# Eleven raw weight slots, ten rounded ones, and a longer lead of the first token tile

## The chip, the cores and the metric

The kernel runs on one core of a Trainium2 chip. The metric is the device time of one execution in microseconds (us), the median of several. The engines go by their names in the profile: PE (TensorE, matmuls; PEld its weight loads), DVE (VectorE), ACT (ScalarE), POOL (GpSimd) and SP (SyncE), whose queue issues the loads of the weights.

## What is computed

Two stacked models share one activation of 256 tokens by 1024 columns. The first has four layers, the second two:

```python
for i in range(DEPTH):                       # 4 layers
    q, k, v, ... = split_cols(x @ w_in[i], ...)          # 3144 or 2560 columns
    mix = attention(q, k, v)                 # selected keys, dilated, or causal blocks
    mo = memory_attention(qm, mk, mv)        # mk, mv = mem_n @ w_mem_kv[i]
    mixed = concatenate([mix, mo]) @ w_out[i]
    x = layer_norm(ALPHA * x + mixed, ...)
    x = layer_norm(ALPHA * x + swiglu(x, w_gate_up[i], w_down[i]), ...)
for l in range(DEPTH_2):                     # 2 layers
    u = rms_norm(x, norm_pre[l]) @ w_in_2[l]             # three attentions on parts of u
    y = gated sum of the three branches @ w_br_a, w_br_b, w_br_c
    x = x + rms_norm(y @ w_out_2[l], norm_post[l])
    x = x + sigmoid(x @ w_ple_gate[l]) * (p[l] @ w_ple_proj[l])
```

All inputs are float32. The result is the last `x`.

## The kernel before

Every product of activations with weights is made of **units**. A unit is up to two row tiles of 128 rows (`UK = 2`) of a column chunk of at most 512 columns. The kernel has 624 of them, numbered in program order. SP loads a unit into one of `RAW = 10` slots; ACT rounds it to float32r in one of `SPLIT = 8` slots (`w_hi`, line 1213); POOL subtracts the rounded from the raw values, in the raw slot itself (`w_lo`, line 1185). PE then makes three products of each row tile: high activations by high weights (L1419), high by low (L1420), low by high (L1426; L1422 where the tile was just turned). The 256 tokens are two tiles of 128, so each unit has two halves on PE, which this text calls the t0 half and the t1 half. A t0 half waits for `w_lo` of its unit; a t1 half comes later in PE's queue.

Slots come free by the t1 half alone: the load of unit n waits for the t1 half of unit n-10, and the rounding of unit n for that of n-8. Unit n's t0 half is planned behind the t1 half of unit n-5 (`LAG = 5`), so t0 runs five units ahead of t1 in the long stages. There are two exceptions. After a norm, the t0 halves of the first `SPLIT` units need no t1 half of the new activations, since the second tile is still being normed. And a chunk that is `closing` (the last one before a norm: the second 512 columns of `w_out`, `w_down`, `w_out_2` and `w_ple_gate_2`) lets the t0 halves of its last two units go one and two units further ahead, so that the first token tile's norm runs on DVE while PE still has t1 halves. After it PE turns the normed rows (L1366) and begins the next weights.

The order on every engine is made when the program is built. `plan()` writes tasks with costs, priorities and what they wait for, and `Plan.arrange()` places them one after the other by earliest begin. Each engine then executes its list in that order, waiting on semaphores. PE's four `acc` banks hold at most two chunks of each token tile, so after a norm at most eight t0 halves of four-unit chunks stand ahead of the first t1 half.

At the seam of `w_gate_up` and `w_down`, the last gate and up chunks have 256 columns (eight narrow units), and the norm's gain and bias are loaded by SP (L1136, L1140) just behind the first load of `w_down`.

Of the kernel before, what the change touches and what calls it, by code (L numbers as in the profile page):

```python
# [42 lines left out]

CHUNK = 512
UK = 2
RAW = 10
SPLIT = 8
LAG = 5
CROSS = 120
FIRST_CONSTANTS = 3  # L50
# [242 lines left out]
class Plan:  # L293
# [135 lines left out]
    def open_chunk(self, weight, k_tiles, acts, spec, fed=((), ()), clear=((), ()), banks=None, hold=((), ()),  # L429
# [8 lines left out]
        for k0 in range(0, k_tiles, UK):  # L438
            n = len(self.units)
            nk = min(UK, k_tiles - k0)  # L440
            u = Unit(n, k0, nk, rows[k0] if rows else k0, ch, weight)
            size = nk * width
            u.load = self.task("SP", "load", u, size * 512 / 300, None,
                               [self.units[n - RAW].mm[1]] if n >= RAW else [], prio=1 if n >= RAW else -3 if n == 0 else -1, lat=2000)
            u.split = self.task("ACT", "split", u, 195 + 0.835 * size, "hi_ready",
                                [u.load] + ([self.units[n - SPLIT].mm[1]] if n >= SPLIT else []),
                                prio=1 if n else -1)
            if n == 0:
                u.low = self.task("DVE", "low", u, 100 + 1.03 * size, "lo_ready_dve", [u.split], prio=-1)
            else:  # L450
                u.low = self.task("POOL", "low", u, 240 + 2.12 * size, "lo_ready", [u.split])
            for t in range(T):
                feed = [self.fed[name][r][base + k0 + i] for r in (range(T) if flip else (t,)) for i in range(nk)]
                u.fed[t] = [k for k in feed if k is not None]
                after = [u.low, *[k.it.hi if k.kind == "take" and not flip else k for k in u.fed[t]]]
                if n:
                    after.append(self.units[n - 1].mm[t])
                if t:
                    after.append(u.mm[0])
                else:  # L460
                    last = n - LAG
                    if n < self.normed + SPLIT:
                        last = min(last, self.normed - 1)
                    if closing and k0 >= k_tiles - 2 * UK:
                        last = len(self.units) - 1 - (k0 - (k_tiles - UK)) // UK - LAG - 2 + 1
                    after += [self.units[last].mm[1]] if last >= 0 else []
                room = None
                if k0 == 0:
                    room = ("acc", banks[t])
                    after += hold[t]  # L470
                u.mm[t] = self.task("PE", "products", (u, t), 3 * nk * pe_cost(width), "mm_done", after,
                                    prio=0.8 + 0.1 * t if closing else 1 + t, room=room)
            self.units.append(u)
            ch.units.append(u)
# [464 lines left out]
def build(nc, a, out):  # L939
# [5 lines left out]
    with ExitStack() as ctx:  # L945
# [8 lines left out]
        with landing:  # L954
            raw = landing.enter_context(nc.sbuf_tensor("raw", [P, RAW, UK, CHUNK], F32))
        rounded = ExitStack()
        with rounded:
            w_lo = rounded.enter_context(nc.sbuf_tensor("w_lo", [P, RAW, UK, CHUNK], F32R))
        ctx.enter_context(nc.sbuf_tensor("raw_or_lo", [P, RAW, UK, CHUNK], F32))
        w_hi = sb("w_hi", [P, SPLIT, UK, CHUNK], F32R)  # L960
        xT_hi = sb("xT_hi", [P, 8, N], F32R)
# [163 lines left out]
        def _(sp):  # L1125
# [16 lines left out]
            def load_unit(u):  # L1142
                if u.u >= RAW:

# [34 lines left out]
        def _(pool):  # L1179
            def low_part(u):  # L1180
                ch, slot, r = u.chunk, u.u % SPLIT, u.u % RAW

# [914 lines left out]
```

How the kernel before makes its waits and increments, by code:

```python
        @block.sync  # L1124
# [1 line left out]
            def load_gain(g):  # L1126
                slot = g.slot
                if g.last is not None:
                    for done in g.last.rest:
                        sp.wait_ge(S["stage"], done.n)
                for done in g.apart:
                    sp.wait_ge(S[done.sem], done.n)
                name, row = g.g
                src = a[name] if row is None else a[name][row]
                to = Y[:, 0, :] if slot else gain[:, 0, :]
                sp.dma_start(to, src.partition_broadcast(P)).then_inc(gain_landed[slot], 16)
                if g.b[0]:
                    name, row = g.b
                    src = a[name] if row is None else a[name][row]
                    sp.dma_start(gain[:, 1, :], src.partition_broadcast(P)).then_inc(gain_landed[slot], 16)
# [1 line left out]
            def load_unit(u):  # L1142
                if u.u >= RAW:
                    sp.wait_ge(S["mm_done"], p.units[u.u - RAW].mm[1].n)
                ch = u.chunk
                src = u.weight[u.row * P:(u.row + u.nk) * P, ch.col:ch.col + ch.width]
                sp.dma_start(raw[:, u.u % RAW, 0:u.nk, 0:ch.width],
                             src.rearrange("(k p) n -> p k n", p=P)).then_inc(unit_landed[u.u % RAW], 16)
# [15 lines left out]
                elif k.kind == "save_rel_rows":  # L1165
                    n = P // REL_PIECES
                    sp.wait_ge(S["rel_rows_made"], 1)
                    sp.dma_start(rel_rows[:, n * k.it:n * k.it + n, :], rel_made.unsqueeze(1)
```

## Time and profile before

| | |
|---|---|
| median of 3 executions | 1910.05 us |
| lowest and highest | 1909.97, 1911.69 us |
| span of the profiled execution | 1906.5 us |
| PE busy | 1865.8 us (98%) |
| POOL busy | 1516.2 us (80%) |
| ACT, DVE busy | 945.2 us (50%), 798.1 us (42%) |
| DMA | 330.54 MB, mean 173 GB/s |

The span runs from the first to the last instruction; the median is 3.5 us longer than it. A matmul's length in the profile reaches past the start of the next one, because matmuls are pipelined, so short waits of PE are partly hidden in its busy time. The number in square brackets at the end of a row of the timeline is the engine's idle time before it and what ended it.

### The profile page before, as it was taken

Reading aid. Unit: us, or ns where it says so; the run is one execution under the profiler, and the core shown is the slowest. Engines: PE = TensorE matmul, PEld = TensorE weight load, DVE = VectorE, ACT = ScalarE, POOL = GpSimd, SP = SyncE. Lnnn points to the kernel's source line nnn. Section 1 sums busy time; section 2 is a strip of 40 time slices with the busy share of each in tenths; the row PEclk is TensorE's granted clock in tenths of the full one; section 3 lists DMA queues with packets and bytes.
Section 4 is the critical chain, followed back from the end, with each engine's and each line's share of the span. In section 5 each row is a group of like instructions: output and inputs, shape, how many; then the busy total and the mean of one; then the engine's idle time right before and its main releaser. Section 6 shows DMA issues by size and latency. Waiting matters only on the chain.

```text
span 1906.5 us, 27403 instructions
## 1 busy us (share of the span) xinstructions
PE 1865.8 (98%) x9610; PEld 1529.7 (80%) x9610; DVE 798.1 (42%) x1933; ACT 945.2 (50%) x1501; POOL 1516.2 (80%) x1330
## 2 busy tenths in 40 slices
PE   8999999999999999999999999999999999999999
PEld 7878888877888887788887778887887887788877
DVE  6774110456111245411056641106857344455534
ACT  4564444454444445444435544434656654555743
POOL 7768979885897977797987779797686887777785
PEclk9999999999999999999999999999999999999999
DMA  8445656555666554465655456655564564556453
GB/s 292 137 146 178 187 164 223 179 176 145 184 193 214 188 172 149 144 188 164 223 150 157 152 166 187 208 169 174 178 182 122 161 209 152 162 170 178 130 173 111
DMA packets 184558, 330.54 MB, mean 173 GB/s; under 512 B 12221, under 2 KB 44521, under 8 KB 184425
## 3 DMA queue, kind: packets, MB, share of 16 engines
q1 hardware_dynamic: 176512, 323.21, 55.0%
q10 hardware_dynamic: 7912, 5.59, 1.0%
q8 instruction: 80, 1.31, 0.3%
q14 instruction: 54, 0.43, 0.1%
HBM read 325.35 MB, written 3.41 MB: 172 GB/s over the span
## 4 chain that ended last, share of the span: by engine, by line
PE 84%; POOL 6%; DVE 4%; DMA 3%; ACT 2%; issue 1%; SPq 0%; DVEq 0%; ACTq 0%
PE acc L1419 24%; PE acc L1420 23%; PE acc L1426 21%; POOL w_lo L1185 6%; PE tps L1366 4%; PE acc L1441 2%; PE acc L1422 2%; PE ops L1483 2%; PE tps L1459 2%; DMA raw<-in_w_down 1%; PE acc L1390 1%; PE acc L1392 1%; PE acc L1391 1%; DMA raw<-in_w_mem_kv 1%; PE ops L1378 1%
## 5 line engine op out<-in xcount | busy, mean ns | idle before, releaser
L1185 POOL TENSOR_TENSOR w_lo<-raw,w_hi 128x512 fp32r<-128x512 f32 (+2 forms) x1242 | 1475.3, 1225 | 349.9 <-ACT w_hi L1213 348.7
L1213 ACT CAST w_hi<-raw 128x1024 fp32r<-128x1024 f32 (+3 forms) x624 | 615.6, 991 | 745.3 <-PE acc L1426 567.2
L1419 PE MATMUL acc<-w_hi,xT_hi 128*128 128x512 f32 (+1 forms) x1808 | 687.1, 384 | 4.9 <-ACT U L1247 2.9
L1420 PE MATMUL acc<-w_lo,xT_hi 128*128 128x512 f32 (+1 forms) x1808 | 666.6, 372 | 0.0
L1426 PE MATMUL acc<-w_hi,xT_lo 128*128 128x512 f32 (+2 forms) x1744 | 505.2, 371 | 0.0
L1419 PEld LDWEIGHTS acc<-w_hi,xT_hi 128*128 128x128 f32 x1808 | 341.4, 189 | 74.6 <-issue 15.2
L1420 PEld LDWEIGHTS acc<-w_lo,xT_hi 128*128 128x128 f32 x1808 | 342.2, 189 | 52.4
L1426 PEld LDWEIGHTS acc<-w_hi,xT_lo 128*128 128x128 f32 x1744 | 317.8, 189 | 58.2 <-DVE xT_lo L1696 1.1
L1756 DVE TENSOR_TENSOR H<-G,acc 128x512 f32<-128x512 f32 (+1 forms) x48 | 30.9, 643 | 335.5 <-PE acc L1426 335.5
L1419 PE MATMUL acc<-w_hi,hT_hi 128*128 128x512 f32 x352 | 139.5, 396 | 3.6 <-POOL w_lo L1185 3.4
L1420 PE MATMUL acc<-w_lo,hT_hi 128*128 128x512 f32 x352 | 137.2, 390 | 0.0
L1426 PE MATMUL acc<-w_hi,hT_lo 128*128 128x512 f32 x352 | 108.5, 389 | 0.0
L1749 DVE SCALAR_TENSOR_TENSOR acc<-x_rows,acc 128x512 f32<-128x512 f32 x32 | 22.2, 694 | 201.5 <-PE acc L1426 175.9
L1267 ACT ACTIVATE L<-L,neg_max 128x128 f32<-128x128 f32 (+2 forms) x208 | 96.2, 464 | 11.2 <-DVE neg_max L1943 8.5
L1419 PEld LDWEIGHTS acc<-w_hi,hT_hi 128*128 128x128 f32 x352 | 66.1, 188 | 21.6 <-issue 8.9
L1419 PE MATMUL acc<-w_hi,sT_hi 128*128 128x512 f32 (+1 forms) x200 | 78.9, 395 | 2.1 <-DVE MKV L1746 1.1
L1426 PEld LDWEIGHTS acc<-w_hi,hT_lo 128*128 128x128 f32 x352 | 66.1, 188 | 14.1
L1420 PE MATMUL acc<-w_lo,sT_hi 128*128 128x512 f32 (+1 forms) x200 | 77.3, 387 | 0.0
L1420 PEld LDWEIGHTS acc<-w_lo,hT_hi 128*128 128x128 f32 x352 | 66.1, 188 | 12.7
L1985 DVE COPY PT<-tps 128x384 f32<-128x384 f32 (+1 forms) x96 | 53.3, 575 | 42.2 <-PE tps L1459 31.1
L1696 DVE TENSOR_TENSOR hT_lo<-tps,hT_hi 128x512 fp32r<-128x512 f32 (+1 forms) x48 | 31.1, 648 | 92.3 <-ACT hT_hi L1221 92.3
L1196 POOL TENSOR_TENSOR L<-L,recips 128x128 f32<-128x128 f32 (+1 forms) x84 | 42.5, 529 | 27.4 <-DVE recips L1973 27.3
(210 smaller groups left out, 1993.5 us busy)
## 6 DMA issues: line engine op xcount, KB each, us to landing
raw<-in_w_gate_up SPq DMA_DIRECT2D x160, 512.0 KB, 3.9
raw<-in_w_in SPq DMA_DIRECT2D x104, 512.0 KB, 3.8
raw<-in_w_down SPq DMA_DIRECT2D x88, 512.0 KB, 3.7
raw<-in_w_out SPq DMA_DIRECT2D x48, 512.0 KB, 3.6
raw<-in_w_in_a SPq DMA_DIRECT2D x32, 512.0 KB, 3.6
raw<-in_w_in_b SPq DMA_DIRECT2D x20, 512.0 KB, 3.7
raw<-in_w_mem_kv SPq DMA_DIRECT2D x16, 512.0 KB, 4.2
raw<-in_w_gate_up SPq DMA_DIRECT2D x32, 256.0 KB, 2.8
```

The lines of the kernel that those rows point to most:

```text
L1185: ins = nc.gpsimd.tensor_tensor(w_lo[:, r, i, 0:ch.width], raw[:, r, i, 0:ch.width], w_hi[:, slot, i, 0:ch.width].bitcast(F32), ALU.subtract)
L1196: ins = nc.gpsimd.tensor_tensor(part, part, by, ALU.mult)
L1213: nc.scalar.copy(w_hi[:, u.u % SPLIT, 0:u.nk, 0:u.chunk.width], raw[:, u.u % RAW, 0:u.nk, 0:u.chunk.width]).then_inc(S["hi_ready"], 1)
L1267: ins = nc.scalar.activation(part, part, ACT.Exp, bias=neg_max[:, slot, c:c + 1], accum_out=sums[:, slot, c:c + 1])
L1366: ins = nc.tensor.transpose(tps[0:width, k.slot[0], P * i:P * i + P], rows(src)[:, t, col:col + width], ident[:])
L1419: nc.tensor.matmul(o, hi[:, tok], wh, start=first_k, stop=False)
L1420: ins = nc.tensor.matmul(o, hi[:, tok], wl, start=False, stop=False)
L1422: ins = nc.tensor.matmul(o, lo[:, tok], wh, start=False, stop=last_k)
L1426: ins = nc.tensor.matmul(acc[:, bank, 0:ch.width], act_tile(ch.acts, u.k0 + i)[1][:, P * t:P * t + P], w_hi[:, u.u % SPLIT, i, 0:ch.width] ...
L1441: ins = nc.tensor.matmul(acc[:, k.slot[m], c], QT[base:base + n, qt, P * t:P * t + P], KT[kbase:kbase + n, kt, 0:c.stop - c.start], start= ...
L1459: ins = nc.tensor.transpose(tps[:, k.slot[0], P * i:P * i + P], lg[:, j, P * i:P * i + P], ident[:])
L1985: v.tensor_copy(PT[:, j, 0:blocks * P], tps[:, s.turn[j].slot[0], 0:blocks * P]).then_inc(S["t_taken"], 1)
```

## The change

Three numbers change: 11 raw slots instead of 10, 10 rounded slots instead of 8, and 1 KB per partition of SBUF set aside for DMA descriptors instead of the default 16 KB, which makes room for them (4 KB of each partition for a slot of either kind). The rule for closing chunks is rewritten: it now holds for all units of such a chunk, and the last one's t0 half is planned behind the t1 half of unit n-9, the one before it behind n-8, then n-7, n-6 and n-5.

```diff
-RAW = 10
-SPLIT = 8
+RAW = 11
+SPLIT = 10
+DMA_SCRATCH = 1024
...
-                    if closing and k0 >= k_tiles - 2 * UK:
-                        last = len(self.units) - 1 - (k0 - (k_tiles - UK)) // UK - LAG - 2 + 1
+                    if closing:
+                        last = min(last, n - max(LAG, SPLIT - 1 - (k_tiles - UK - k0) // UK))
...
-    nc = bacc.Bacc("TRN2", target_bir_lowering=False, num_devices=1)
+    nc = bacc.Bacc("TRN2", target_bir_lowering=False, num_devices=1, dynamic_dma_scratch_size=DMA_SCRATCH)
```

No instruction is added or taken away; the lists of all engines are ordered anew. Lines are numbered one higher in the new kernel. Three places show it.

**SP, the start of the program.** `raw` is a unit's slot, `in_w_mem_kv` the weights of the memory keys and values, `masks` to `sinks` constants. Before:

```order
10 L1148 DMA raw<-in_w_in_a 128x2x512 x2
11 L1148 DMA raw<-in_w_mem_kv 128x2x512 x2
12 L1164 DMA masks<-in_c_masks 128x1536
13 L1164 DMA knorm<-in_idx_kn_g 128x2x64
...
19 L1164 DMA sinks<-in_sw_sinks 128x16
20 L1148 DMA raw<-in_w_mem_kv 128x2x512 x2
```

Now:

```order
10 L1149 DMA raw<-in_w_in_a 128x2x512
11 L1149 DMA raw<-in_w_mem_kv 128x2x512 x3
12 L1165 DMA masks<-in_c_masks 128x1536
13 L1165 DMA knorm<-in_idx_kn_g 128x2x64
...
19 L1165 DMA sinks<-in_sw_sinks 128x16
20 L1149 DMA raw<-in_w_mem_kv 128x2x512
```

The third unit of `w_mem_kv` is now issued ahead of the eight constants; the fourth stays behind them. One more unit of `w_in_a` also stands ahead of the load of `mem`.

**PE, the end of `w_down` in layer 0.** `x_rows` are the first token tile's normed rows being turned, `hT` the activations of `w_down`, `MKV` the memory keys of the next layer. Before:

```order
1273 L1366 MATMUL tps<-ident,x_rows 128x128 x8
1274 L1419 MATMUL acc<-w_hi,hT_hi 128x512
...
1283 L1426 MATMUL acc<-w_hi,hT_lo 128x512 x2
1284 L1366 MATMUL tps<-ident,MKV 128x128 x4
```

Now:

```order
1259 L1367 MATMUL tps<-ident,x_rows 128x128 x8
1260 L1420 MATMUL acc<-w_hi,hT_hi 128x512
...
1279 L1427 MATMUL acc<-w_hi,hT_lo 128x512 x2
1280 L1367 MATMUL tps<-ident,MKV 128x128 x4
```

A half is five rows. Two t1 halves stood between the turned rows and the end of the stage, and now four do. Five stand between the last t0 half and the turned rows both times: seven t1 halves in all before, nine now. The same holds for the other three `w_down` and the two `w_out_2`; `w_out` of layer 0 has eight instead of seven, and `w_out` of layers 1 to 3 keep six, five and five.

**DVE, the end of `w_ple_gate_2` in the first of the two layers.** L1860 to L1863 add a chunk of one token tile into its bank, L1610 begins the first tile's norm, L1849 writes its normed rows. Before:

```order
1296 L1860 TENSOR_TENSOR acc<-acc,U 128x512
1297 L1862 TENSOR_TENSOR acc<-acc,x_rows 128x512
...
1302 L1860 TENSOR_TENSOR acc<-acc,U 128x512
1303 L1862 TENSOR_TENSOR acc<-acc,x_rows 128x512
1304 L1863 BN_STATS stats<-acc 128x6
1305 L1610 BN_AGGR small<-stats 128x2
...
1316 L1849 SCALAR_TENSOR_TENSOR tmp<-acc,small,gain 128x512 x2
1317 L1860 TENSOR_TENSOR acc<-acc,U 128x512
```

Now:

```order
1291 L1861 TENSOR_TENSOR acc<-acc,U 128x512
...
1294 L1861 TENSOR_TENSOR acc<-acc,U 128x512
1295 L1863 TENSOR_TENSOR acc<-acc,x_rows 128x512
1296 L1864 BN_STATS stats<-acc 128x6
1297 L1611 BN_AGGR small<-stats 128x2
...
1308 L1850 SCALAR_TENSOR_TENSOR tmp<-acc,small,gain 128x512 x2
1309 L1697 TENSOR_TENSOR xT_lo<-tps,xT_hi 128x4x128 x2
1310 L1861 TENSOR_TENSOR acc<-acc,U 128x512
```

Of the second token tile, one chunk's addition stood ahead of the first tile's norm, and now none does. On PE, the t0 halves of `w_ple_proj_2` and of all of `w_ple_gate_2` (ten units, 520 to 529) now stand ahead of the t1 half of unit 520; before, five t1 halves stood ahead of unit 528 and one more ahead of 529, so that four were left behind the last t0 half, where ten are now. The turned rows stand behind the fifth of the ten.

## Rows read from the trace of the kernel before

**Rows 1.** The page, 1: busy time of each engine.
```profile
PE 1865.8 (98%) x9610; PEld 1529.7 (80%) x9610; DVE 798.1 (42%) x1933; ACT 945.2 (50%) x1501; POOL 1516.2 (80%) x1330
```

**Rows 2.** The waits of PE, whole span: total us, times, longest.
```profile
PE tps L1366 <- DVE tmp L1849: 5.2, 2, 2.6
PE acc L1419 <- POOL w_lo L1185: 4.9, 15, 1.6
...
PE tps L1459 <- DVE L L2012: 4.2, 3, 1.7
```

**Rows 3.** Timeline of PE, end of w_down, layer 0: start, length, line.
```profile
343.13 0.61 PE L1426 MATMUL acc<-w_hi,hT_lo 128*128 128x512 f32 x2
...
344.49 0.61 PE L1426 MATMUL acc<-w_hi,hT_lo 128*128 128x512 f32 x2
...
349.03 1.05 PE L1366 MATMUL tps<-ident,x_rows 128*128 128x128 f32 x8
```

**Rows 4.** Timeline of PE, end of w_gate_up, layer 0: two neighbouring t1 halves.
```profile
277.67 0.62 PE L1426 MATMUL acc<-w_hi,xT_lo 128*128 128x512 f32 x2
...
279.77 0.62 PE L1426 MATMUL acc<-w_hi,xT_lo 128*128 128x512 f32 x2
```

**Rows 5.** The chain, 280 to 360 us: start, length, what.
```profile
280.42 6.54 DMA raw<-in_w_down
288.11 22.55 POOL w_lo L1185 x18
...
340.97 0.25 PE acc L1419
```

**Rows 6.** POOL by line, 288.2 to 343.1 us; PE's waits, 280 to 345 us.
```profile
L1185 POOL TENSOR_TENSOR w_lo<-raw,w_hi 128x512 fp32r<-128x512 f32 x44 | 55.0, 1294 | 2.2 <-ACT w_hi L1213 2.2
...
PE acc L1419 <- POOL w_lo L1185: 1.0, 4, 0.4
```

**Rows 7.** Timeline of DVE and PE, end of layer 3.
```profile
1284.97 0.70 DVE L1749 SCALAR_TENSOR_TENSOR acc<-x_rows,acc 128x512 f32<-128x512 f32 x1 [13.58 <-PE acc L1426]
...
1309.56 1.41 DVE L1849 SCALAR_TENSOR_TENSOR tmp<-acc,small,Y 128x512 f32<-128x512 f32 x2
...
1297.01 1.93 PE L1366 MATMUL tps<-ident,tmp 128*128 128x128 f32 x8 [2.56 <-DVE tmp L1849]
...
1310.56 1.18 PE L1366 MATMUL tps<-ident,tmp 128*128 128x128 f32 x8
```

**Rows 8.** PE by windows of 8 us: busy (count), granted clock, DMA.
```profile
1294.00:1302.00 8.00, 5.44 (x22) 0.79 0.57 208
1596.00:1604.00 8.00, 5.29 (x19) 0.80 0.55 194
```

**Rows 9.** Timeline of DVE and PE, end of the first w_ple_gate_2.
```profile
1591.46 0.70 DVE L1860 TENSOR_TENSOR acc<-acc,U 128x512 f32<-128x512 f32 x1 [10.94 <-ACT acc L1247]
...
1598.47 1.41 DVE L1849 SCALAR_TENSOR_TENSOR tmp<-acc,small,gain 128x512 f32<-128x512 f32 x2
...
1590.69 0.62 PE L1426 MATMUL acc<-w_hi,xT_lo 128*128 128x512 f32 x2
...
1599.37 1.29 PE L1366 MATMUL tps<-ident,tmp 128*128 128x128 f32 x8 [2.62 <-DVE tmp L1849]
...
1609.38 1.04 PE L1366 MATMUL tps<-ident,tmp 128*128 128x128 f32 x8
```

**Rows 10.** Timeline of PE, the start: the fourth of its products.
```profile
45.57 0.47 PE L1419 MATMUL acc<-w_hi,mT_hi 128*128 128x512 f32 x1 [1.57 <-POOL w_lo L1185]
```

**Rows 11.** Timeline of DVE and POOL in the differential attentions.
```profile
1342.26 0.75 DVE L2012 SCALAR_TENSOR_TENSOR L<-L,recips 128x128 f32<-128x128 f32 x2
...
1652.59 2.86 DVE L2012 SCALAR_TENSOR_TENSOR L<-L,recips 128x128 f32<-128x128 f32 x2
...
1652.61 5.22 POOL L1185 TENSOR_TENSOR w_lo<-raw,w_hi 128x512 fp32r<-128x512 f32 x4 [2.17 <-ACT w_hi L1213]
```

**Rows 12.** The page, 3: the queue of the weights; packets, MB, share of time.
```profile
q1 hardware_dynamic: 176512, 323.21, 55.0%
```

## The prediction

> **What bounds the kernel now.** I read the page first: PE is busy for 1865.8 of 1906.5 us [rows 1], so only its waits and its clock can be won. Then the waits of PE over the whole span, grouped by what ended them [rows 2]: DVE's `tmp` 5.2 us in two waits, POOL's `w_lo` 4.9 us in 15, the attention's `L` 4.2 us in three. Then the timeline around the seams that the change reorders, and the granted clock there. Since the next matmul starts before the shown end of the one ahead, a shown wait is some 0.16 us longer in truth (0.39 us shown against starts 0.23 us apart, in the timeline around the row of [rows 10]).
>
> The unit of account is a half of a 512-wide unit on PE: 344.49 - 343.13 = 1.36 us [rows 3], so 2.72 us a unit, while POOL makes its `w_lo` in 55.0 / 44 x 2 = 2.50 us [rows 6]. POOL gains only 0.22 us a unit on PE. That small margin is what decides the sum: where the new order wants `w_lo` earlier than before, POOL must have started earlier by as much.
>
> **The start, -0.9 us.** PE waits 1.57 us for POOL before the third unit of `w_mem_kv` [rows 10], 1.8 us in truth, and its load stands behind eight constants. It now stands ahead of them; the fourth stays behind. The fourth is wanted about one t0 half of this narrow product, 0.9 us, later than the third was, so I take 1.8 - 0.9 = 0.9 us as still waited for. Bounds: 0 if the constants only push the wait to the fourth unit whole, -1.8 if it goes. The extra load of `w_in_a` ahead of `mem` is covered, since DVE takes up `mem` late.
>
> **End of `w_down` in layers 0 to 2, +0.6 us each.** What starts POOL: the load of the second `w_down` unit was issued at 280.42, right behind the t1 half of the unit ten before it, took 6.54 us, and after ACT's rounding POOL works from 288.11 on [rows 5] without a pause worth the name: 2.2 us idle in the 55 [rows 6]. With an eleventh slot the load waits for the t1 half one unit earlier. Neighbouring t1 halves start 2.10 us apart here (279.77 - 277.67 [rows 4]; the units are narrow), so the whole row of POOL comes 2.1 us earlier. The four waits of PE at the head of `w_down` (1.0 us shown, 1.6 in truth [rows 6]) then go. At the tail, the last unit's t0 half starts at 341.03 now (the chain has PE at it from 340.97 [rows 5]), 0.4 us after its `w_lo`, so just in time. The new order has two more t1 halves behind it: wanted at 341.0 - 1.6 - 2 x 1.36 = 336.7, while POOL can give it at 341.0 - 2.1 = 338.9. So a wait of 2.2 us appears there. The turned rows then end at 338.9 + 1.36 + 9 x 1.36 + 0.9 = 353.4, if all nine t1 halves (five and four) stand behind the last t0 half as the order has it. The same sum for now is 341.0 + 1.36 + 7 x 1.36 + 0.9 = 352.8: +0.6 us, three times, +1.8 in all. The norm of the first tile ends well ahead in both. Bounds: -1.6 each if POOL keeps up (the head's waits go, no tail wait), +2.7 each if POOL doesn't start earlier at all (rival B).
>
> **End of layer 3, -2.1 us.** Here the norm is longer than the t1 halves behind it. PE waits 2.56 us for `tmp`, and again it turns rows at 1310.56 just when DVE has the second tile's `tmp` of 1309.56; DVE began the first tile at 1284.97 [rows 7] and works on without a pause. The window 1294 to 1302 has a granted clock of 0.79 [rows 8], that is, some 3.4 us of it at the lower level of 1.2 GHz and 1.7 us lost. Wait and clock cost 2.56 + 0.16 + 1.7 = 4.4 us, but DVE's row of work ends them both, and all that moves it is the end of the t0 halves, which comes earlier by POOL's 2.1 us. So -2.1 us; the two further t1 halves behind the last t0 half (2 x 1.36 = 2.7 us) fill the gap and more. Bounds: 0 (POOL doesn't start earlier) and -2.7.
>
> **First `w_ple_gate_2`, -3.0 us.** The gap is 2.62 us in front of the turned rows at 1599.37 [rows 9], and the clock of 1596 to 1604 is 0.80 [rows 8]: 2.62 + 0.16 + 1.6 = 4.4 us lost. From DVE's first addition at 1591.46, right behind the last t0 half, to PE's turning it is 8 us, of which four t1 halves (5.4 us) cover the most. Now ten t1 halves stand behind the last t0 half, five of them ahead of the turned rows: 6.8 us of cover. The gap shrinks to 8.1 - 6.8 = 1.3 us, too short to lower the clock if it goes as with the waits of 1.7 us (no window shows a drop there). 4.4 - 1.4 = 3.0 us won. The second turning at 1609.38 hangs on the last t1 half; it is wanted some five t0 halves after the first new one (6.9 us) and is ready 7 to 8 us after the last t1 half, so it takes back at most 1 us. Bounds: -4.4 (gap closes, as DVE no longer serves another chunk first) and -1.5 (POOL gives the last two units late: it has ten `w_lo` to make with PE using t0 halves alone, at 1.36 us each against its 2.50).
>
> **Other seams, 0.** `w_out` in layers 1 to 3 keeps its order, and the second `w_ple_gate_2` and the two `w_out_2` have no such gap today. New banks or reads cost nothing.
>
> **The scratch of 1 KB, 0.** It is a reservation. All 323 MB of weights go by a queue of the kind hardware_dynamic [rows 12], and GpSimd issues no load. If it did slow the loads, each `w_down` load would land later than 6.54 us after its issue, and the forecast would become rival B. Nothing in it can gain.
>
> **Attentions, 0, between -4 and +4.** PE's list is the same in layers 1 and 2; in the differential attention the scores start a little earlier and fewer t1 halves cover what follows. POOL, two units ahead, meets DVE at other moments. That matters: a pair of L2012 takes 0.75 us at 1342.26, but 2.86 us at 1652.59, when POOL has a row of `w_lo` from 1652.61 on [rows 11]. Each pair costs 2.1 us more when it collides; 3 of 8 do so by the timeline (a fourth in part), and PE's 4.2 us for `L` [rows 2] hang on them. The Trainium skill ("SBUF — State Buffer", "Who interferes with whom") says that the shared port pair of DVE and GpSimd is an exclusive lock; by that rule a DVE operation with two SBUF inputs is held up whole while a GpSimd instruction holds the lock, and the trace agrees (2.86 against 0.75 us). That makes rival C.
>
> **Sum.** -0.9 + 1.8 - 2.1 - 3.0 = -4.2 us against the span of 1906.5, so 1902.3. The median is 3.5 us above the span; 1905.8 is the predicted time. About 0.2% (3.8 us) is what a measurement of this kernel can tell from no change, so that the bound of faster lies at 1906.2, hardly above it.
>
> **The rivals.**
>
> A, POOL keeps up at the ends of `w_down`. For it: it has 80% of the span as busy time, and two more rounded slots let it take in whatever idle time it has earlier in `w_gate_up`. Against it: raw slots, not rounded ones, set when `w_down` lands [rows 5]. -1.6 x 3, -0.9 to -1.8, -2.1, -4.4: -12 to -13, and the middle between this and the forecast is 1901; the full case 1897.5.
>
> B, the slower one: POOL gets no head start in `w_down`. The transfer of 6.54 us [rows 5] lies beside other loads and is issued one slot sooner only to queue; if it lands at 287 as before, the tail's last `w_lo` comes at 340.6 as before, and behind its t0 half there are now nine halves instead of seven: +2.7 us in each of three layers, +8.1. The end of layer 3 gives 0, the gate -2, the start -0.9: 1910.05 + 5.2 = 1915.3. It decides against me from the point where POOL's start moves by less than 1.5 us (the forecast's three ends then cost over 3.6 us together). Against it: the load is issued at once when its slot comes free, today.
>
> C, collisions in the attentions. Two more pairs of L2012 that meet POOL's row, on the path, are +4.2 us and eat the gain: 1909 to 1911. For it: which ones meet depends on a microsecond, and the margins of PE's turning behind them are small. Against: it can as well go the other way.
>
> D, hardly an effect: the change doesn't do at the gate what its order says, because there, as in layer 3 [rows 7], DVE's row of both norms sets when PE goes on: the second turning at 1609.38 [rows 9] stays, and the cover of ten halves is filled for nothing. Then -0.9 + 1.8 - 2.1 = -1.2 us, 1908.9, or up to 1911 if layer 3 stays too.
>
> **How the numbers follow.** Forecast 0.40 (1903 to 1908.5, 60% of it below 1906.2), A 0.20 (1897 to 1903), C 0.18, D 0.08, B 0.14 (1914 to 1917). Faster: 0.24 + 0.20 = 0.44, and 0.01 for C going the other way, 0.45. Slower 0.14, same the remaining 0.41. The range of 1898.0 to 1912.0 leaves out B and the low end of A, nearly 2 in 10.
>
> **What would show it.** In the new trace the load of the second `w_down` unit lands about 2.1 us earlier against the t1 halves of `w_gate_up`, PE's four waits at the head of `w_down` are gone, and two or so of 1 us or more stand ahead of the last two t0 halves of it. The gap of 2.56 us in layer 3 is under 1 us, that of 2.62 us about 1.3, and the granted clock is 1.00 in both places. The wait in the start is 1 us or less. The prediction is wrong in its main step if POOL's start in `w_down` moves by less than 1.5 us, or if no wait appears at its tail; it is wrong in size if the differential attentions' waits for `L` move by over 2 us.

## The result, and the profile after

The changed kernel takes 1915.43 us (median of 18 executions, 1909.5 to 1918.5) and the kernel before 1909.28 us (18 executions, 1907.1 to 1912.0): 1.0027 of the time before, with a 95% interval of 1.0021 to 1.0034. It is slower by some 5 to 6 us, beyond the 0.2% that the prediction set as its bound. The profiled execution has a span of 1914.9 us, 8.4 us above the 1906.5 us of before. It took 1916.74 us, 1.3 us more than the median. A time is here 1.8 us above the span of the same execution, so the one of before took some 1908.3 us, 1.0 us less than its median. That is why the spans differ by 8.4 us and the medians by 6.1. The size of each seam below holds for the profiled execution only.

The page of the kernel after, busy time, which answers to [rows 1]:

```profile
PE 1869.1 (98%) x9610; PEld 1531.1 (80%) x9610; DVE 804.1 (42%) x1933; ACT 943.5 (49%) x1501; POOL 1514.3 (79%) x1330
```

And its waits of PE over the whole span (total us, times, longest), which answer to [rows 2]:

```profile
PE acc L1420 <- POOL w_lo L1186: 7.9, 16, 1.7
...
PE acc L1420 <- DVE MKV L1747: 2.5, 3, 1.7
...
PE tps L1460 <- DVE L L2013: 2.3, 2, 1.3
PE acc L1427 <- DVE xT_lo L1697: 2.0, 1, 2.0
PE acc L1420 <- ACT xT_hi L1222: 1.7, 3, 0.7
...
PE tps L1367 <- DVE sT_lo L1697: 1.5, 2, 0.8
```

The wait for `tmp` (5.2 us before) has shrunk to 0.3 us as intended, but the wait for POOL's `w_lo` has grown from 4.9 to 7.9 us, and others have come or grown: `xT_lo` and `sT_lo` were not in the list of before, and `xT_hi` had 0.2 us. PE does the same work; what the change bought at two places it gave back at others.

To see where, I compared the two traces at the end of the t1 half of the same unit, stage by stage. A t1 half's end is in PE's timeline as the last row of L1427 (L1426 before) of that unit. Each number is how much that end has moved (us, + is later) against the same end in the kernel before, over the stage alone. The last four columns are experiments told below. The borders are units behind which the order of halves is the same in all columns. The columns come from one execution each: against the medians of their kernels, the profiled one of the slots alone is 2.3 us long, that of the gate alone 1.3 us short, that of the late gains 1.2 and of both 2.8 us short.

| stage | after | slots alone | gate alone | late gains | gate and late gains |
|---|---|---|---|---|---|
| start to end of `w_out`, layer 0 | +2.6 | +4.1 | +1.3 | +2.0 | +1.3 |
| end of `w_down`, layer 0 | +2.5 | +1.7 | +1.9 | -1.2 | -2.0 |
| attention and `w_out`, layer 1 | +1.2 | +1.3 | +0.4 | +0.4 | +0.4 |
| end of `w_down`, layers 1 and 2 | +1.1 | -1.6 | -2.1 | -2.2 | -3.5 |
| attention and `w_out`, layers 2 and 3 | -0.6 | -0.9 | -0.4 | -0.7 | -0.8 |
| end of layer 3 | +0.7 | -0.9 | -1.1 | -0.7 | -2.0 |
| first differential attention, to `w_br_c` | -0.1 | -0.1 | +0.9 | +0.1 | 0.0 |
| the two `w_out_2` | +3.8 | -0.1 | 0.0 | +3.8 | 0.0 |
| first `w_ple_gate_2` | -4.4 | -4.5 | -4.5 | -4.0 | -4.9 |
| second differential attention, to `w_br_c` | +1.6 | +9.1 | -0.9 | -1.0 | -1.1 |
| sum, with rests of 0.1 or less | +8.4 | +8.1 | -4.5 | -3.5 | -12.8 |

**End of `w_down`, layer 0.** The chain of waits of the kernel after, 276 to 292 us, and in layer 1, 590 to 604 us:

```profile
278.78 0.37 SPq L1149
279.25 1.27 SPq L1137
280.56 0.43 SPq L1141
281.04 8.35 DMA raw<-in_w_down
289.41 1.06 ACT w_hi L1214
290.54 2.51 POOL w_lo L1186 x2
...
594.58 6.38 DMA raw<-in_w_down
600.99 1.05 ACT w_hi L1214
602.11 2.56 POOL w_lo L1186 x2
```

In layer 1 it went as I worked out from [rows 4, 5]: the second load of `w_down` is issued one narrow t1 half earlier and takes 6.38 us. In layer 0 it is issued earlier too, but takes 8.35 us instead of 6.54, and SP needs 1.27 us to issue the gain (L1137) where it needs 0.41 elsewhere. POOL's head start of 2.1 us shrinks to 0.1. PE's timeline shows it at the head and at the tail:

```profile
293.20 0.47 PE L1420 MATMUL acc<-w_hi,hT_hi 128*128 128x512 f32 x1 [1.67 <-POOL w_lo L1186]
...
343.17 0.47 PE L1420 MATMUL acc<-w_hi,hT_hi 128*128 128x512 f32 x1 [0.87 <-POOL w_lo L1186]
```

The second of them is the last t0 half of `w_down`, with the wait at the tail that the prediction expected. In the kernel before the same half begins at 340.81, in PE's timeline:

```profile
340.81 0.41 PE L1419 MATMUL acc<-w_hi,hT_hi 128*128 128x512 f32 x1
```

So it starts 2.4 us later in the span, of which 2.6 us had been lost earlier: it came 0.2 us earlier than before, not 2.1, and the nine t1 halves follow it.

**End of layer 3**, timelines of PE and DVE, which answer to [rows 7]:

```profile
1301.33 1.26 PE L1367 MATMUL tps<-ident,tmp 128*128 128x128 f32 x8
1303.15 0.47 PE L1420 MATMUL acc<-w_hi,xT_hi 128*128 128x512 f32 x1 [0.55 <-issue]
...
1306.36 1.22 PE L1427 MATMUL acc<-w_hi,xT_lo 128*128 128x512 f32 x2 [2.05 <-DVE xT_lo L1697]
...
1305.61 1.29 DVE L1697 TENSOR_TENSOR xT_lo<-tps,xT_hi 128x512 fp32r<-128x512 f32 x2
```

And PE by windows of 8 us (busy, count, granted clock, DMA share, GB/s), as in [rows 8]:

```profile
1304.00:1312.00 8.00, 5.95 (x20) 0.79 0.22 85
```

The gap of 2.56 us before the turned rows is gone. But DVE now writes the low parts of those rows (`xT_lo`) at 1305.61, behind the whole inverse root of the second tile, 4 us after they were turned. Before, the first of the two was written at 1298.77, between the second tile's statistics and that root:

```profile
1298.77 0.67 DVE L1696 TENSOR_TENSOR xT_lo<-tps,xT_hi 128x512 fp32r<-128x512 f32 x1
```

Now PE waits 2.05 us two matmuls further on, and the granted clock is 0.79 there instead of in front of the turning.

**The two `w_out_2`**, PE's timeline, the first of them:

```profile
1566.97 0.66 PE L1367 MATMUL tps<-ident,Y 128*128 128x128 f32 x4 [0.74 <-DVE sT_lo L1697]
1568.30 0.50 PE L1420 MATMUL acc<-w_hi,xT_hi 128*128 128x512 f32 x1 [0.68 <-ACT xT_hi L1222]
```

The longer lead puts the t0 halves of the closing chunk ahead of the last t1 half of `w_br_c` (unit 511 in the first layer). It completes the second token tile's `Y`, which `w_out_2` itself needs. So its turning and its rounding no longer have work of PE beside them: 0.74 + 0.68 us and twice 0.16 for the pipelined records, in each of the two layers.

### The profile page after: what moved, and what is told of

Read it like the earlier page. It is cut to its first block, busy times and chain, and to the rows that moved or that the text cites. A ratio compares the mean times of both kernels' runs of the same rounds, so it can differ in the third digit from the quotient of the medians.

```text
span 1914.9 us, 27397 instructions
## 1 busy us (share of the span) xinstructions
PE 1869.1 (98%) x9610; PEld 1531.1 (80%) x9610; DVE 804.1 (42%) x1933; ACT 943.5 (49%) x1501; POOL 1514.3 (79%) x1330
## 4 chain that ended last, share of the span: by engine, by line
PE 77%; POOL 12%; DVE 5%; DMA 3%; ACT 2%; issue 1%; SPq 0%; DVEq 0%; ACTq 0%
PE acc L1420 22%; PE acc L1421 21%; PE acc L1427 19%; POOL w_lo L1186 12%; PE tps L1367 4%; PE acc L1442 2%; PE acc L1423 2%; PE ops L1484 2%; PE tps L1460 2%; DMA raw<-in_w_down 1%; PE acc L1391 1%; PE acc L1393 1%; PE acc L1392 1%; DMA raw<-in_w_mem_kv 1%; PE ops L1379 1%
## 5 line engine op out<-in xcount | busy, mean ns | idle before, releaser
L1420 PE MATMUL acc<-w_hi,xT_hi 128*128 128x512 f32 (+3 forms) x1808 | 686.9, 384 | 6.0 <-ACT U L1248 2.0
L1421 PE MATMUL acc<-w_lo,xT_hi 128*128 128x512 f32 (+3 forms) x1808 | 666.8, 372 | 0.0
L1427 PE MATMUL acc<-w_hi,xT_lo 128*128 128x512 f32 (+2 forms) x1744 | 506.3, 372 | 2.1 <-DVE xT_lo L1697 2.0
L1427 PEld LDWEIGHTS acc<-w_hi,xT_lo 128*128 128x128 f32 x1744 | 318.3, 189 | 60.7 <-DVE xT_lo L1697 3.8
L1427 PE MATMUL acc<-w_hi,hT_lo 128*128 128x512 f32 x352 | 108.6, 390 | 0.0
L1427 PEld LDWEIGHTS acc<-w_hi,hT_lo 128*128 128x128 f32 x352 | 66.1, 188 | 14.2
L1421 PEld LDWEIGHTS acc<-w_lo,hT_hi 128*128 128x128 f32 x352 | 66.1, 188 | 12.6
```

Of the source, the lines that this page charges most:

```text
L1420: nc.tensor.matmul(o, hi[:, tok], wh, start=first_k, stop=False)
L1421: ins = nc.tensor.matmul(o, hi[:, tok], wl, start=False, stop=False)
L1427: ins = nc.tensor.matmul(acc[:, bank, 0:ch.width], act_tile(ch.acts, u.k0 + i)[1][:, P * t:P * t + P], w_hi[:, u.u % SPLIT, i, 0:ch.width] ...
```

## What the experiments asked

Each result below is the median, its ratio to the kernel before measured beside it, and the 95% interval of that ratio. The theories have letters of their own, which are not those of the prediction's rivals. Theory C said that the longer lead costs the time and the slots help. Theory S said that the slots cost it, by another order in the start and in the attentions. Later came H (POOL's start in `w_down`, set by the loads ahead of it), F (the long load in layer 0), P (DVE and POOL in the attention), G (what wins at `w_ple_gate_2`) and D (DVE's order in layer 3).

**The slots alone.** The old closing rule with everything else new:

```diff
-                    if closing:
-                        last = min(last, n - max(LAG, SPLIT - 1 - (k_tiles - UK - k0) // UK))
+                    if closing and k0 >= k_tiles - 2 * UK:
+                        last = len(self.units) - 1 - (k0 - (k_tiles - UK)) // UK - LAG - 2 + 1
```

> Eleven raw and ten rounded slots and the small scratch, with the old rule for closing chunks. Theory C (the longer lead costs the time, the slots help): about 3 to 6 us below the kernel before; the load of the second w_down unit is issued 2.1 us earlier, PE's waits at the head of w_down go and none comes at its tail; the two gaps of 2.6 us before the turned rows stay. Theory S (the slots disturb the start and the attentions): 4 us or more above the kernel before, with the lost time in the first 130 us and in the attentions.

1914.11 us, 1.0023 (1.0015 to 1.0031). By its time, theory S. But the table splits it: the slots win at `w_down` in layers 1 to 3 (-2.6 together) and at the gate (-4.5), and lose 4.1 us in the start and 9.1 us in one attention. The profiled execution is the longest of twelve (1908.4 to 1916.4 us), so these two losses may be smaller in the others. What the attention's loss is, its trace tells, DVE, POOL and PE in the second differential attention:

```profile
1643.83 7.68 DVE L1876 SCALAR_TENSOR_TENSOR U<-U,subln 128x512 f32<-128x512 f32 x1 [0.47 <-ACT U L1248]
...
1635.20 15.76 POOL L1186 TENSOR_TENSOR w_lo<-raw,w_hi 128x416 fp32r<-128x416 f32 x14
...
1652.52 0.80 PE L1442 MATMUL acc<-KT,QT 64*128 64x128 f32 x4 [5.21 <-DVE L L1930]
```

An operation of 0.7 us takes 7.68: it ends at 1651.51, 0.55 us behind the end of POOL's row of fourteen (1635.20 + 15.76 = 1650.96). What stands behind it in DVE's queue keeps PE's scores waiting 5.21 us, and the granted clock falls with it (PE by windows of 8 us):

```profile
1648.00:1656.00 8.00, 3.48 (x13) 0.63 0.00 0
```

In the kernel before, the same operation starts at 1643.86 and takes 0.79 us: POOL, two units less ahead, works there in pairs (1641.99 to 1644.10, 1644.71 to 1646.83) with a pause of 0.6 us between them, and the operation ends 0.55 us behind the first pair.

**The scratch alone.**

```diff
+DMA_SCRATCH = 1024
...
+    nc = bacc.Bacc("TRN2", target_bir_lowering=False, num_devices=1, dynamic_dma_scratch_size=DMA_SCRATCH)
```

> Only the DMA scratch of 1 KB, all else as in the kernel before. Theories C and S: no change, within 1 us. A rival, that the smaller scratch slows the loads: 3 us or more above the kernel before, with loads that take longer than 6.5 us at the start of w_down.

1908.71 us, 0.9997 (0.9988 to 1.0005): nothing, as both theories said.

**Ten raw slots.** The changed kernel with `RAW = 10`:

> As the changed kernel, but with ten raw slots. Theory C, with POOL's start as what decides in w_down: the load of the second w_down unit is issued 2.1 us later than in the changed kernel, so the wait at the tail of each w_down grows by about 2 us and the kernel is 6 to 9 us slower than the changed one. Theory S: 2 us or more faster than the changed kernel, since the eleventh slot's early loads are what disturbs the start.

1922.59 us, 1.0073 (1.0061 to 1.0085): 7 us slower than the changed kernel, as theory C had said, but not by its reason. The second `w_down` load is issued 2.1 us later, as said, and in layer 0 takes 6.59 us. But the planner, which sees POOL late, keeps the old order at the tail of `w_down`, so that the two further t1 halves aren't there. The ends of `w_down` in layers 0 to 2 lose 0.5 us each, in layers 1 and 2 no more than with eleven slots and in layer 0 less; the end of layer 3 loses 1.5 us (0.7 with eleven). The loss against the changed kernel lies at the two `w_out_2` (2.3 us more), in the first differential attention (1.9) and around the attentions of layers 1 and 3. So the right total proved nothing. An experiment that changes a number of the planner changes all seams, and only the comparison seam by seam can be used.

**The longer lead in `w_ple_gate_2` alone.** `w_out`, `w_down` and `w_out_2` go by the old rule (their calls say `closing="short"`):

```diff
+                    if closing == "short":
+                        if k0 >= k_tiles - 2 * UK:
+                            last = len(self.units) - 1 - (k0 - (k_tiles - UK)) // UK - LAG - 2 + 1
-                    if closing:
+                    elif closing:
```

> As the changed kernel, but the longer lead only in w_ple_gate_2; w_out, w_down and w_out_2 keep the old rule. Theory C: the 4.4 us won at the first w_ple_gate_2 stay and the losses at w_down (+0.5 to +2.6 each) and at the two w_out_2 (+1.9 each) go: 6 to 10 us below the kernel before. Theory S: the start and the attentions still lose 4 us and more, so that it is at best level with the kernel before.

1905.15 us, 0.9979 (0.9970 to 0.9988). Against the changed kernel the two `w_out_2` win 3.8 us, `w_down` in layers 1 to 3 some 5 us. So the lead costs there, which is theory C; layer 0's `w_down` stays slow (+1.9), so the lead is not its cause.

**The gain and bias behind the eleventh unit of `w_down`**, in the otherwise unchanged new kernel:

```diff
-        g = p.gain("ln2_g", "ln2_b", l, up.units[-1].load)
         spec = [(c, n, "residual", c) for c, n in column_chunks(0, D)]
         down = lin(w["w_down"][l], FF // P, "h", spec[:1])
+        g = p.gain("ln2_g", "ln2_b", l, down[0].units[10].load)
```

> The changed kernel with one edit: the norm's gain and bias for the end of a layer are loaded behind the eleventh unit of w_down instead of behind its first one (1 MB less ahead of the second unit). Theory H (the longer lead in w_down costs time because POOL's start, set by the landing of the second unit, is too late for it): that unit lands 2 us or more earlier after its issue, and 3.5 us or more earlier in layer 0, the waits of 0.85 us at the tail of each w_down and those at its head go, and 6 to 9 us are won against the changed kernel (1906 to 1909). Rival (PE is held by the nine t1 halves and DVE's order, not by POOL): the landing moves, the time by less than 2 us.

1906.04 us, 0.9981 (0.9972 to 0.9990), some 9 us less than the changed kernel. The waits of PE from 260 to 360 us of this kernel:

```profile
PE acc L1420 <- POOL w_lo L1186: 0.5, 1, 0.5
```

And of the changed kernel from 280 to 360 us:

```profile
PE acc L1420 <- POOL w_lo L1186: 3.1, 5, 1.7
```

Theory H holds: with 1 MB less ahead of it the second load of `w_down` takes 4.2 us instead of 8.35, and the four ends win 3.7, 1.6, 1.6 and 1.4 us against the changed kernel, 8.3 of the 11.9 us between the two profiled executions (9.4 between the medians). At the tails some 0.5 us of wait is left where I had expected none.

**Both.** The longer lead in `w_ple_gate_2` alone and late gains:

> The kernel with the longer lead in w_ple_gate_2 alone, and the gain and bias loads behind the eleventh unit of w_down. By theory H the waits at the head of w_down go in all layers, and the 1.9 us lost at layer 0 too: 3 to 6 us below 1905.2, that is 1899 to 1902. By the rival, no change from 1905.2.

1898.38 us, 0.9938 (0.9925 to 0.9950). No wait for `w_lo` is left at either end of any `w_down`.

**PE's instructions moved by 12 matmuls.** A repeat of the first turns, in the changed kernel:

```diff
+                first = [] if k.n > 1 else [*enumerate(b.moves)] * 3
-                for i, (src, t, col, width) in enumerate(b.moves):
+                for i, (src, t, col, width) in [*first, *enumerate(b.moves)]:
```

> The changed kernel with PE's first four turns of x repeated three times, which computes nothing new and moves all that follows in PE's instruction stream by 12 matmuls and their weight loads. Theory F (in layer 0 the second w_down load takes 8.4 instead of 6.5 us because a 16 KB transfer of PE's instructions starts in the same 0.1 us as SP's issue of the gain): that transfer starts some 2.5 us earlier, SP's issue of the gain takes 0.4 instead of 1.3 us, the load some 6.5 us, and w_down of layer 0 ends 1.5 to 2 us earlier against the t1 halves of w_gate_up. Rival (the eleventh slot itself makes the queue fuller): the load stays over 8 us.

Queue q8, of the kind instruction, has 80 packets of 16 KB in every trace. PE executes 9610 matmuls and as many weight loads, so one packet for every 240 of its instructions, and their times move with PE's list. I take them for PE's instructions; which engine a packet serves is in no view. The DMA queues of the changed kernel, 279.0 to 279.6 us:

```profile
q8 instruction: 1, 0.02, 9.9%
```

And SP's queue in the kernel with the repeated turns:

```profile
280.57 0.37 SPq L1149 DMA_DIRECT2D raw<-in_w_down  x1
281.04 0.41 SPq L1137 DMA_DIRECT2D gain<-in_ln_g  x1
281.49 0.43 SPq L1141 DMA_DIRECT2D gain<-in_ln_b  x1
282.67 2.48 SPq L1149 DMA_DIRECT2D raw<-in_w_down  x2
```

Here the packet starts at 278.59, 2.0 us ahead of the issue of the first `w_down` load (280.57), instead of at 279.18, 0.4 us behind it (278.78). The gain's issue is back to 0.41 us, the load to 6.63 us (7.16 to 9.30 in the kernels where they coincide), and the end of `w_down` in layer 0 wins 1.8 us. The sizes agree over all kernels with the gain in its old place: where the packet starts 1.9 to 2.0 us ahead of the first load's issue, the second load takes 6.54, 6.66, 6.59 and 6.63 us; at the same time, 7.16; 0.2 to 0.4 us behind it, 8.81, 9.30 and 8.35. The kernel as a whole is slower (1919.02), and its end of layer 3 bears theory F out once more. There a packet now starts 0.20 us behind the issue of the first `w_down` load (1226.30), and the same thing happens that has gone from layer 0. SP's queue, the chain of waits, and PE's waits from 1220 to 1330 us:

```profile
1226.77 1.10 SPq L1137 DMA_DIRECT2D gain<-in_ln_g  x1
...
1228.40 8.54 DMA raw<-in_w_down
...
PE acc L1421 <- POOL w_lo L1186: 3.1, 5, 1.7
```

In the changed kernel this load takes 6.36 us and the waits are 1.2 us in three; the end of layer 3 costs +4.1 here and +0.7 there. The start, +4.4, holds PE's twelve further matmuls too.

**The start by the old slots.** Ten raw and eight rounded slots up to unit 47, on top of both:

```diff
+            raw, split = (10, 8) if n < 48 else (RAW, SPLIT)
...
-                               [self.units[n - RAW].mm[1]] if n >= RAW else [], prio=1 if n >= RAW else -3 if n == 0 else -1, lat=2000)
+                               [self.units[n - raw].mm[1]] if n >= raw else [], prio=1 if n >= raw else -3 if n == 0 else -1, lat=2000)
```

(and the same with `split` for the rounding and the rule after a norm)

> As the kernel with the longer lead in w_ple_gate_2 alone and late gain loads, but the first 48 units keep the waits of ten raw and eight rounded slots. Theory S (the 1.3 us that the start up to w_out of layer 0 loses with the new slots comes from the new order there): the start is level with the kernel before and the time 1 to 1.5 us lower than without the edit. Rival (the start depends on the chip, not on the order): no change.

1896.76 us, 0.9931 (0.9919 to 0.9944): 1.6 us less in the median, and the start of the profiled execution at +0.5 instead of +1.3. The direction is as expected; the intervals of the two overlap, so the total alone doesn't settle it.

The other traces do. Up to the end of the first attention there are only two orders in all but two of the kernels, the same on every engine. In the five other kernels with the old one, the start ends at -0.6 to +0.5 against the kernel before. In the six with the new one (the changed kernel, the slots alone with and without POOL's added wait below, the gate alone, the late gains, both) it ends at +1.3 to +4.1. So the new order costs the start 1.3 us or more. The rest of up to 2.8 us isn't the order's, since it is the same in all six. In the two with over 3 us, PE waits 1.1 us more for a `w_lo` at 58.8 us; why POOL is late in these executions stays open.

**One more wait on POOL**, in the kernel with the slots alone:

```diff
+                if u.u == 550:
+                    gained = [k for k in order["DVE"] if k.kind == "stage" and k.it.fn == "gain_z" and k.it.layer == 1]
+                    pool.wait_ge(S["stage"], min(k.n for k in gained))
```

> The kernel with the new slots and the old closing rule (1914.1), with one wait more on POOL: its w_lo of unit 550 waits until DVE has finished the gate's scaling for the first token tile in the second differential attention. Theory P (DVE's operation takes 7.7 us there because POOL works on w_lo in a row): it takes 0.7 to 1.3 us, PE's wait of 5.2 us before the scores goes, POOL stands still for 1 us or so, and 5 to 8 us are won (1906 to 1909). Rival (the operation is long for another reason, its data or its place): it stays over 5 us, or moves with DVE's next operation, and so does the time.

1908.83 us, 1.0000 (0.9991 to 1.0009), 5.3 us less (4.4 by the two ratios). DVE and POOL in it:

```profile
1644.10 0.69 DVE L1879 SCALAR_TENSOR_TENSOR U<-U,subln 128x512 f32<-128x512 f32 x1 [0.32 <-ACT U L1251]
...
1635.80 8.42 POOL L1189 TENSOR_TENSOR w_lo<-raw,w_hi 128x416 fp32r<-128x416 f32 x8
1644.87 10.04 POOL L1189 TENSOR_TENSOR w_lo<-raw,w_hi 128x512 fp32r<-128x512 f32 x8 [0.66 <-DVE U L1879]
```

A wait added makes the kernel faster: POOL stands still for 0.66 us, DVE's operation takes 0.69 instead of 7.68, PE's wait of 5.21 us is down to 0.4, and the stage costs 2.7 instead of 9.1 us. Theory P is shown: POOL's row of `w_lo` holds DVE's operation up. The rule of the Trainium skill that the prediction cited ("SBUF — State Buffer", "Who interferes with whom") says that the shared port pair is an exclusive lock; the trace agrees with it (0.69 against 7.68 us), though that a hold lasts over six `w_lo` in a row is more than the rule tells. And the operation doesn't always have to wait for a pause. In the changed kernel it takes 1.53 us at 1649.57, in the middle of a row of POOL that goes on to 1655.98; there one `w_lo` takes 1.71 instead of 1.28 us. What decides between the two stays open.

**Late gains alone**, in the kernel before:

> The kernel before (ten raw slots, eight rounded, old closing rule, 16 KB scratch), with the gain and bias loads behind the eleventh unit of w_down. Theory H: the second unit of w_down lands about 2.5 us earlier, so that the waits of 1.6 us at the head of w_down go in four layers and no more: 5 to 7 us below the kernel before, 1903 to 1905. Rival (eight rounded slots hold POOL's start back even then): less than 3 us won.

1902.82 us, 0.9968 (0.9956 to 0.9980), 5.7 us less, by 1.5, 1.1, 0.8 and 1.8 us at the four ends. One edit of the loads' order, with no slot more, does more than the change was able to.

**The old closing rule on top of the fastest.** Of the change only slots and scratch are left:

> As the fastest so far (1896.8: new slots from unit 48 on, late gain loads, longer lead in w_ple_gate_2 alone), with the old closing rule there too, so that of the change only the slots and the scratch are left. Theory G (the 4.4 us at the first w_ple_gate_2 come from the ten rounded slots, which let all ten t0 halves go ahead, and not from the closing rule): the seam of w_ple_gate_2 still wins 4 to 4.5 us. The time is level with 1896.8 unless DVE and POOL meet otherwise in the second differential attention, which by the run with the slots alone may cost up to 9 us. Rival (the closing rule makes the gain): the seam wins less than 2 us.

1904.39 us, 0.9978. The seam of the first `w_ple_gate_2` still wins 4.4 us. Theory G holds in its main point, that the slots win the seam and the closing rule adds nothing to it. The detail was another than I had expected: with the old rule not all ten t0 halves go ahead. Eight do, three t1 halves follow, then the last two t0 halves, so that seven t1 halves are left behind them instead of the four of before, five of them ahead of the turned rows. DVE no longer adds a chunk of the second tile before the first tile's norm, so its row up to `tmp` is 2.1 us shorter, and the gap is gone as with ten.

The 7.6 us that this kernel is slower (9.0 by the two ratios) are for the most part the second differential attention again, 7.1 us in the traces (DVE's operation 7.39 us). The same holds for what "the lead in `w_ple_gate_2`" won against the slots alone: 10.0 of the 12.6 us between their two sums lie in that attention, where the operation takes 1.33 us instead of 7.68. Another 2.8 us lie in the start, where the two kernels have the same order. The rule itself won nothing at its own seam.

**Layer 3 with the longer lead and DVE in the right order:**

```diff
+            second = [k for k in p.tasks if k.kind == "stage" and k.it.fn == "layer_norm_scale" and k.it.t == 1][-1]
+            second.after.append(p.fed["x"][0][7])
```

(and `closing=True` for `w_down` in layer 3, `"short"` in the others)

> As the fastest so far (1896.8), and at the end of layer 3 the longer lead in w_down, with DVE made to write both low parts of the first token tile's turned rows before it begins the second tile's statistics. Theory D (in the changed kernel the longer lead closes the gap of 2.56 us there, but DVE writes the low parts 4 us late and the wait moves behind the turned rows, 2.05 us and a lower clock): PE's wait before the turned rows is under 0.5 us, the one behind them under 0.5 us, the granted clock stays 1.00, and 1 to 2.5 us are won. Rival (DVE's row of the two norms sets the end anyway): the second turning waits instead, and less than 0.7 us are won.

1896.13 us, 0.9926 (0.9912 to 0.9939). PE's timeline in it:

```profile
1287.24 1.28 PE L1373 MATMUL tps<-ident,tmp 128*128 128x128 f32 x8
1289.04 0.47 PE L1426 MATMUL acc<-w_hi,xT_hi 128*128 128x512 f32 x1 [0.53 <-issue]
...
1300.86 0.63 PE L1373 MATMUL tps<-ident,tmp 128*128 128x128 f32 x4 [0.70 <-DVE tmp L1856]
```

And the window around the turning:

```profile
1288.00:1296.00 8.00, 7.47 (x35) 1.00 0.44 163
```

No wait ahead of the turned rows, none for `xT_lo` behind them, a granted clock of 1.00: the end of layer 3 wins 2.4 us more than in the kernel without the edit. What is left is a wait of 0.70 us at the second turning, where the rival had put it. Theory D is shown for the seam. The medians differ by 0.6 us only (1.0 by the two ratios), less than their intervals tell apart, so whether all 2.4 us reach the end is open.

## Why the prediction was wrong

It forecast 1905.8 us with 1898 to 1912 as the range. The time is 1915.4, outside it and on the other side. In the spans it is +8.4 instead of -4.2 us. Of these some 12.6 us, 3.8 lie in the two `w_out_2`, 3.5 in the start, 2.8 in the end of layer 3, 1.9 in layer 0's `w_down` and 2.1 in the attentions; the first gate gave 1.4 more than forecast. Rival B's total, 1915.3, is within 0.2 us of the median by luck: its mechanism acted in one layer of three.

- **Start, forecast -0.9, +2.6 to the end of `w_out` in layer 0 (with the attention).** The wait for a `w_lo` of `w_mem_kv` [rows 10] did shrink, from 1.57 to 0.95 us (at 46.93). How near that is to the forecast says little: kernels with the same order there have 0 to 0.95 us, those with the old one 0.56 to 1.75. The step that failed was to look at that wait alone. The new slot numbers reorder the whole first attention, and small waits came there (0.82 us for `mT_hi` at 51.16; 0.73, 0.43 and 0.57 us between 100 and 122 us, where two of 0.51 and 0.17 stood). Old order against new, in twelve traces, shows a cost of 1.3 us or more; the spread from +1.3 to +4.1 us at one and the same order is not explained.
- **End of `w_down`, forecast +0.6 each.** In layers 1 and 2 it is +0.56 and +0.51 in the profiled execution: the head start of 2.1 us, a wait at the tail (0.85 us in layer 1, where I had 2.2) and the nine halves. For layer 0 the prediction read the last t0 half's start as 341.03 where the trace has 340.81, which moves both of its sums alike. In layer 0 it is +2.5, which is rival B's price of +2.7 and its mechanism (no head start), but for one layer and not three. The step that failed there was to keep 6.54 us for the load issued one slot sooner: it took 8.35, and POOL's head start was 0.1 us. The cause lies in a place at which I had not looked: a packet of instructions in the same microsecond as the issue of the loads.
- **End of layer 3, forecast -2.1, was +0.7.** The t0 halves did end 2.3 us earlier, and the gap went. The step that failed was that DVE "works on without a pause", taken as if its order were fixed. I had compared PE's list there and not DVE's: `xT_lo` moved behind the second tile's root, and gave the wait and the clock back. Repairing that order gave -2.4 us in the last experiment. Rival D had allowed for layer 3 staying as it is, though by another mechanism.
- **First `w_ple_gate_2`, forecast -3.0, was -4.4**, the bound named for a closed gap, and by the reason named with it. The gap in front of the first tile's turned rows is gone, since DVE's row is 2.1 us shorter without the other chunk; 0.26 us of wait is left at the second turning. I had put that reason in the bound and not in the sum. And it is the slots that bring it, not the closing rule.
- **"Other seams, 0" was the dearest step.** The two `w_out_2` cost +3.8. I had listed them as having nine halves instead of seven and given them no cost, since no gap stood there before. But the longer lead pulled t0 halves ahead of a t1 half that feeds the same chunk's second tile. What a lead takes its halves from must be asked, as well as what it covers.
- **Attentions, forecast 0 within 4 us; rival C at 0.18.** The second differential one cost +1.6 us here and +9.1 with the slots alone. The mechanism of C was right, and its size too small in that one trace: I had priced a collision as one `w_lo` more for each operation (2.1 us a pair), while an operation can also be held up until POOL's whole row has ended. Layer 1's attention with `w_out` cost +1.2 us; why stays open.
- **The scratch, 0**, was right.
- **The median 3.5 us above the span.** In all other profiled executions the time is 1.8 to 2.2 us above the span of the same execution. The rest of the 3.5 was that the profiled execution of before was a short one.

My chance of 0.14 for slower was tied to rival B alone. The losses were several of 1 to 2.5 us, each in a seam whose order had changed, against a gain that was sure in one place.

## What to carry to other kernels

When a change moves numbers from which an order is made, compare the new order on every engine at every seam, and give a seam without a gap a cost too: halves put ahead of others come from somewhere. If a queue of loads sets when an engine can start, look first at what stands ahead of the load that it waits for; 1 MB of gain and bias moved behind eleven loads won 5.7 us alone, and some 12 us together with the slots and the lead at the gate. And compare experiments stage by stage at the same unit: totals of reordered kernels differ by some 7 us through one collision. First look whether a stage's order differs at all between the two: here a start in the same order took between 1.3 and 4.1 us more than before, so a difference in one pair of traces isn't yet the effect of the edit.

## What the runs showed of the hardware

- DVE and POOL hold each other up, and what a collision costs depends on how they meet. In a long row of `w_lo`, DVE's small operations each take as long as one `w_lo`: 1.12 to 1.25 us for 128x4 elements, eleven of them in the latent norm of the first differential attention (0.16 us is the shortest of the kind in the same trace). One of 128x512 was held for 7.68 and 7.39 us, both times until 0.55 us behind the end of POOL's row, and for 1.53 us in the middle of a row in the changed kernel. The kernel after, DVE and POOL:

```profile
1386.94 1.21 DVE L1546 SCALAR_TENSOR_TENSOR small<-small 128x4 f32<-128x4 f32 x1
...
1381.84 18.82 POOL L1186 TENSOR_TENSOR w_lo<-raw,w_hi 128x512 fp32r<-128x512 f32 x15 [3.58 <-ACT w_hi L1214]
```

- A 16 KB packet of the instruction queue that starts with the issue of a load or up to 0.45 us behind it goes with 0.67 to 1.71 us for SP's next issue instead of some 0.4, if that one follows within 0.6 us. From 60 us on, so it is in all 15 such places of the 14 traces, while without a packet 415 of 420 such issues take under 0.6 us. Where the next issue comes later, 199 of 202 beside a packet are under 0.6 us too. At the head of layer 0's `w_down` the next 512 KB load then took 0.6 to 2.8 us longer. It hits or misses by where an engine's list stands. The 18 executions of the changed kernel spread over 9 us, the 18 of before over 5; whether this is why was not measured.
- After a wait of 2.05 us right behind the turned rows the granted clock fell to 0.79 over 8 us, as it did after waits of 2.6 us in front of them; with waits of 0.5 and 0.7 us it stayed at 1.00. Beside the wait of 5.21 us it was 0.63.
